# Dilated column scores: the mask is added by VectorE on the way out of the bank instead of by a TensorE product inside it

## What is computed

```
def dilated_window_attention(q, k, v, window, dilation):
    ...
    s = jnp.einsum('bnqhd,bnkhd->bnhqk', qs, kb, preferred_element_type=F32) * scale
    ...
    valid = (dist >= 0) & (dist <= n_back) & (u_key >= 0)
    s = jnp.where(valid[None, :, None], s, -jnp.inf)
    m = jnp.max(s, axis=-1, keepdims=True)
    p = jnp.exp(s - m)
    denom = jnp.sum(p, axis=-1, keepdims=True)
    o = jnp.einsum('bnhqk,bnkhd->bnqhd', (p / denom).astype(v.dtype), vb)
    lse = (m + jnp.log(denom))[..., 0]
```

## Time and profile before

| | us |
|---|---|
| median of 3 runs | 1390.65 |
| lowest, highest | 1389.37, 1392.71 |
| the profiled execution | 1388.89 |
| its span, first to last instruction | 1387.1 |
| PE busy in it | 1329.0 |
| DVE, ACT, POOL busy | 498.7, 667.5, 693.8 |
| mean granted PE clock, as a share of 2.4 GHz | 0.985 |

### The profile page before, as it was taken

One profiled execution on the slowest core, in us unless ns is written; L12 is line 12 of the kernel. 1 busy time (PEld: TensorE's weight loads), 2 busy tenths in 40 slices (PEclk: granted clock), 3 DMA queues, 4 the chain that ended last, 5 costly groups with the idle time before them and its releaser, 6 DMA issues. The chain is left out here.

```text
span 1387.1 us, 17627 instructions
## 1 busy us (share of the span) xinstructions
PE 1329.0 (96%) x6234; PEld 1037.4 (75%) x6234; DVE 498.7 (36%) x765; ACT 667.5 (48%) x1233; POOL 693.8 (50%) x571
## 2 busy tenths in 40 slices
PE   7999899988999999999999998999889999999998
PEld 6778778865677788887877786886556768888876
DVE  4675332343341222223338724114442412222221
ACT  5554423566354644554445542247644445455431
POOL 3676522354242467767447753224432425776662
PEclk9999999999999999999999999999999999999999
DMA  7553311121222243444355522112122213344432
GB/s 222 159 131 102 87 39 39 39 54 39 61 59 56 48 123 101 110 108 114 101 163 146 130 84 69 39 31 54 46 49 50 69 46 88 102 108 113 107 114 84
DMA packets 210031, 120.78 MB, mean 87 GB/s; under 512 B 9752, under 2 KB 200472, under 8 KB 209944
## 3 DMA queue, kind: packets, MB, share of 16 engines
q1 hardware_dynamic: 209944, 119.66, 32.9%
HBM read 107.04 MB, written 6.29 MB: 82 GB/s over the span
## 5 line engine op out<-in xcount | busy, mean ns | idle before, releaser
L1633 POOL TENSOR_TENSOR w_lo<-w_raw,w_hi 128x512 fp32r<-128x512 f32 (+1 forms) x404 | 501.5, 1246 | 623.5 <-ACT w_hi L1165 574.6
L747 PE MATMUL dense<-h_hi,w_hi 128*128 128x512 f32 x1168 | 502.8, 430 | 2.2 <-DVE h_lo L1346 2.1
L747 PE MATMUL dense<-h_hi,w_lo 128*128 128x512 f32 x1168 | 460.1, 394 | 0.0
L747 PE MATMUL dense<-h_lo,w_hi 128*128 128x512 f32 x1168 | 459.8, 394 | 0.0
L747 PEld LDWEIGHTS dense<-h_hi,w_hi 128*128 128x128 f32 x1168 | 222.4, 190 | 69.6 <-issue 21.9
L1165 ACT ACTIVATE w_hi<-w_raw 128x512 fp32r<-128x512 f32 (+1 forms) x401 | 232.7, 585 | 62.8 <-PE dense L747 62.6
L747 PEld LDWEIGHTS dense<-h_lo,w_hi 128*128 128x128 f32 x1168 | 222.3, 190 | 53.8 <-issue 14.4
L747 PEld LDWEIGHTS dense<-h_hi,w_lo 128*128 128x128 f32 x1168 | 221.3, 189 | 48.6
L1439 DVE TENSOR_TENSOR sig<-dense,x_rstd_row 128x512 f32<-128x512 f32 x48 | 33.2, 692 | 208.0 <-issue 122.8
L1441 DVE TENSOR_TENSOR raw<-dense,x_rstd_row 128x512 f32<-128x512 f32 x80 | 55.1, 688 | 122.4 <-PE dense L747 98.9
L1218 ACT ACTIVATE sig<-sig 128x512 f32<-128x512 f32 x48 | 30.3, 632 | 123.1 <-DVE sig L1439 123.1
(11 more groups left out here) (261 smaller groups left out, 1916.4 us busy)
## 6 DMA issues: line engine op xcount, KB each, us to landing
w_raw<-in_w_in SPq DMA_DIRECT2D x292, 256.0 KB, 2.9
w_raw<-in_w_out SPq DMA_DIRECT2D x32, 256.0 KB, 2.8
x_scratch<-v_dil SPq DMA_DIRECT2D x16, 256.0 KB, 3.4
w_raw<-in_w_mem_kv SPq DMA_DIRECT2D x16, 256.0 KB, 2.7
v_dil<-x_scratch SPq DMA_DIRECT2D x16, 256.0 KB, 2.8
turned<-normed SPq DMA_DIRECT2D x48, 64.0 KB, 2.4
inv_den<-o_norm SPq DMA_DIRECT2D x48, 64.0 KB, 2.4
silu_z<-in_mem SPq DMA_DIRECT2D x4, 512.0 KB
```

The costliest lines, as they stand in the source:

```text
L747: return nc.tensor.matmul(o, lhsT, rhs, start=start, stop=stop, skip_group_check=True)
L1633: pool.tensor_tensor(w_lo[:, g % SPLIT_SLOTS, c], w_raw[:, g % RAW_SLOTS, c], f(w_hi[:, g % SPLIT_SLOTS, c]), ALU.subtract).then_inc(w_lo_ ...
```

## The change

PE no longer issues the mask products of the dilated `col` steps; `less_maximum` ends the group and signals `col_done`. A new step on DVE waits for the `probs` slot and for `col_done`, adds the mask to the bank's scores and writes the sum into the `probs` slot: two additions per head for c = 0 (256 and 256 columns) and c = 1 (256 and 128), one of 512 for c = 2 and 3. It signals `s_masked`, which now frees the score bank. ACT waits for `s_masked` and exponentiates the slot in place. The other branches and the `row` steps keep their mask products.

```
             elif s[0] == "col":
-                score_users.append((s, p_ready, s[1:]))
+                score_users.append((s, s_masked if s[1] == DIL else p_ready, s[1:]))
                 probs_users.append((s[1:], pv_done, s[1:]))
...
-                                    less_maximum(h_, bank_[:, at:at + end - j * P], negmax_r[:, j * P:end])
-                                pairs_of = lambda ap: ap.rearrange("p (a b) -> p a b", b=P)
-                                if c == 0:
-                                    last = masked(bank_[:, :].rearrange("p (i a b) -> p i a b", i=2, b=P),
-                                                  causal_band[:, None, :, :].to_broadcast((P, 2, 2, P)))
-                                else:
-                                    masked(pairs_of(bank_[:, 0:2 * P]), causal_band)
-                                    last = masked(bank_[:, 2 * P:3 * P], rc(M_CAUSAL))
-                                last.then_inc(col_done.sem, 1)
+                                    last = less_maximum(h_, bank_[:, at:at + end - j * P], negmax_r[:, j * P:end], stop=True)
+                                    if i == 1:
+                                        last.then_inc(col_done.sem, 1)
...
-                                less_maximum(h_, by_class, strided)
-                                masked(by_class, times(rc(M_CAUSAL if g == 1 else M_COMB), STRIDE)).then_inc(col_done.sem, 1)
+                                less_maximum(h_, by_class, strided, stop=True).then_inc(col_done.sem, 1)
...
-                        wait(act, probs_ring.before(key))
-                        act.wait_ge(*col_done.of(key))
+                        if b == DIL:
+                            act.wait_ge(*s_masked.of(key))
+                        else:
+                            wait(act, probs_ring.before(key))
+                            act.wait_ge(*col_done.of(key))
...
+                        elif b == DIL:
+                            act.activation(dst, dst, ACT.Exp).then_inc(p_ready.sem, 1)
...
+                    elif kind == "col" and s[1] == DIL:
+
+                        b, h, c = key = s[1:]
+                        bank_, to = (ap.rearrange("p (a b) -> p a b", b=P)
+                                     for ap in (R[score_ring.slot(s)][:, :], probs[:, probs_ring.slot(key), :]))
+                        banded = f(rconst[:, M_CAUSAL - 2:M_BAND - 1:M_BAND - M_CAUSAL, :])
+                        causal, comb = f(rc(M_CAUSAL)), f(rc(M_COMB))
+
+                        def masked(blocks, mask):
+                            return dve.tensor_tensor(to[:, blocks, :], bank_[:, blocks, :], mask, ALU.add)
+
+                        wait(dve, probs_ring.before(key))
+                        dve.wait_ge(*col_done.of(key))
+                        if c < 2:
+                            masked(slice(0, 2), banded)
+                            last = masked(slice(2, 4), banded) if c == 0 else masked(slice(2, 3), causal[:, None, :])
+                        else:
+                            mask = causal if c == 2 else comb
+                            last = masked(slice(0, STRIDE), mask[:, None, :].to_broadcast((P, STRIDE, P)))
+                        last.then_inc(s_masked.sem, 1)
```

More of the change, by code:

```diff
@@ L484, in build @@
         p_ready = signal("p_ready", of_kind("col"))
+        s_masked = signal("s_masked", [k for k in of_kind("col") if k[0] == DIL])
         pv_done = signal("pv_done", of_kind("pv"))
@@ L805, in operand @@
                     return h_hi[:, kt, :], h_lo[:, kt, :]
-                def times(ap, n):
-                    return ap[:, None, :].to_broadcast((P, n, P))
                 def qk_there(kind, branch, idx):
@@ L996, in masked @@
                             return mm(o, rc(IDENT), blocks, stop=True)
-                        causal_band = rconst[:, M_CAUSAL - 2:M_BAND - 1:M_BAND - M_CAUSAL, :]
                         if b == FOX:
```

## The result

The changed kernel takes **1381.21 us** (median of 4 runs, 1380.15 to 1381.95), the kernel before beside it 1390.01 (4 runs, 1388.83 to 1392.71): 0.9946 of the time before, with a 95% interval of 0.9929 to 0.9964. That is 8.8 us by the medians. The four runs before are on the high side: 32 later runs of the same kernel have a median of 1388.96, 7.8 us above the change. One further run of the kernel before took 6352 us; it is left out everywhere. The profiled execution took 1380.15 us with a span of 1378.4, against 1388.89 and 1387.1.

The account below looks back on a forecast made before the run. The prediction took PE's own work to bound the kernel: 7.7 us of masks less waits of 0.65 and 0.4 gives 6.7 us gained, from the runs' median 1390.65 to 1383.9, range 1380.0 to 1388.3.

Parts of the forecast that it names:

- A mask's price: Column stages on PE: each removed mask saves its start-to-start step, 32 x 0.24 = 7.7 us less.
- Those at half clock at full-clock price: Six of the 32 mask places show 0.40 or 0.41 us at 1.2 GHz; counted at 0.24 like the others.
- Price of the additions: DVE's new additions in the column stages: 0.69 us for 512 columns, 0.41 for 256, 0.28 for 128.
- The hop's waits: PE waits for the longer DVE-then-ACT chain at pair 0, 0.6 to 0.7 us in all, and pair 6, 0.4 in all.
- reaches pair 1 at 197.99: Pair 0, layer 0: PE gets from the delayed `pv` to pair 1 in 1.56 us, at 197.99 instead of 198.12.
- Sum at equal clock: Whole kernel, clock unchanged: 7.7 us of masks less waits of 0.65 and 0.4 gives 6.7 us gained.
- the same mean clock of about 0.92: Column stages: PE's mean granted clock stays at about 0.92, as in the kernel before.
- A stretch's price: Column stages: each 3.4 us stretch at 1.2 GHz costs half its length, 1.7 us.
- Two stretches fewer, 1380.5: Rival: the shift moves the clock's falls and two fewer come, ending at 1380.5 us; chance 0.08.
- Slower, by the clock: Rival: without masks PE does less per time, the clock falls more often, six more falls give 1394.2 us; chance 0.05.
- The additions' high price: Rival: DVE's additions cost 2.4 times as much, waits take 6.1 us, ending at 1390.0; shares chance 0.11.
- hidden products: Rival: removed masks had been hidden behind weight loads, so PE gains nothing, ending at 1390; shares chance 0.11.

Follow-up runs that it names:

- no_masks: The changed kernel without masks for the dilated column scores and without DVE's additions, ACT reading the bank with scores scaled by 0.001: 1379.47 us.
- add_twice: The changed kernel with every DVE addition made twice, the second behind a signal of the first: 1386.61 us.
- room: The changed kernel with two empty places per layer moved from the end, one behind pair 0, one ahead of pair 6: 1377.17 us.
- split: The changed kernel with the 24 64-row products of pairs 2, 3 and 7 issued in two halves, one in each head's step: 1380.05 us.
- room_split: The changed kernel with both the two moved empty places per layer and the halved 64-row runs of pairs 2, 3 and 7: 1375.51 us.

## Why the prediction was right, and where it was off

Forecast was 1383.9 with 1380.0 to 1388.3; it came to 1381.2. Of the 2.7 us between them 1.7 have nothing to do with the change: the forecast subtracts its gain from 1390.65, the median of three runs, and 32 later runs have 1388.96. The gain itself, 6.7 forecast, is 7.6 between the means of the 32 runs and of the change's ten, 6.6 of it at equal clock. That 6.6 meets 6.7 so well is partly luck: in the stages the masks gave less and the waits took more than was forecast. One step was wrong, the clock that was to stay.

- **What bounds the stage**: right. Taking work from PE pays nearly in full (`no_masks`), more work on DVE costs nothing but delay, at the same two places and a little at a third (`add_twice`).
- **A mask's price**: 32 x 0.24 = 7.7 us forecast; by the stages of `no_masks` 7.1, or 0.22 each, by its runs at equal clock 7.7. "Those at half clock at full-clock price" holds well enough: had the six counted 0.40, the sum would be 8.6. By the 131 ns that the prediction took from the Trainium skill, "TensorE: Matmul & The Clock Gate", section "Back-to-back issue gap", it would be 4.2 us; the removal decides for the trace's step. The same section of the Trainium skill gives about 216 ns for a single product of 512 columns, and that agrees with the trace's 0.22.
- **Price of the additions**: right, 0.69, 0.42 and 0.28 us.
- **The hop's waits**: the places are right. Pair 6 waits 0.20 and 0.26 (0.2 forecast). At pair 0 the step "reaches pair 1 at 197.99" failed: it took 1.56 us from the `pv` to pair 1, and they are 1.73. In layer 1 the wait is 0.84 and not 0.62, although the order is the same: there the `pv` starts 0.26 us behind the end of ACT's exponential (871.47 to 871.73), in layer 0 0.10; why, no run shows. Against the 0.46 us that its masks free, pair 0 gives up 0.54 and 0.71, where 0.33 was forecast; with pair 6 that makes 1.7 us over both layers for the sum's 1.05.
- **Sum at equal clock**: 6.7 forecast. The stages give 2 x (58.1 - 55.45) = 5.3 (about 7.1 less 1.7), or 6.0 with 1.1 us for a stretch; the runs at equal clock give 6.6. What is missing may lie outside the stages, but the two executions of the kernel before differ there by 2 us once carried to an equal count (1262.6 us with five stretches, 1262.0 with six), which is too much to tell. All say that the forecast was near, and none that it was too low.
- **The clock**: forecast "the same mean clock of about 0.92"; it was 0.94. This is the step that failed, and the reason that the gain is larger than forecast. Before, a stage had 3.0 stretches, with the change 1.8 (six stages): 1.17 x 1.4 = 1.6 us per stage, 3.3 in all. Most of it doesn't stay: over all runs the mean clock went from 0.9834 to 0.9846, which is about 3.4 us less at 1.2 GHz in an execution, one stretch and not the 2.3 that the stages have lost, and worth 1.1 us; the others came back outside the stages. The balance is 2 x (62.32 - 58.02) = 8.6 us in the stages, and 7.6 between the means of all runs.
- **A stretch's price**: 1.7 forecast as half of 3.4 us, measured 1.1 to 1.4. Part of what falls into a stretch loses nothing. These are rows of the kernel before, the second head's strided subtraction, the mask behind it and the next product, all in pair 2: first in layer 0 at full clock, then in layer 1 within a stretch, with its clock. The subtraction takes 0.45 us and 0.46 from start to start, the mask 0.25 and 0.41.

```profile
207.39 0.62 PE L747 MATMUL score<-negmax_r,pick 128*128 128x512 f32 x1
207.84 0.42 PE L747 MATMUL score<-rconst 128*128 128x512 f32 x1
208.09 0.81 PE L747 MATMUL acc<-probs,v_dil 128*128 128x256 f32 x4
...
885.24 0.65 PE L747 MATMUL score<-negmax_r,pick 128*128 128x512 f32 x1
885.70 0.61 PE L747 MATMUL score<-rconst 128*128 128x512 f32 x1
886.11 1.48 PE L747 MATMUL acc<-probs,v_dil 128*128 128x256 f32 x4
```
```profile
885.00:886.00 1.00, 1.00 (x4) 0.77 (x3) 0.00 (x0) 0.46 (x1) 0.00 (x0) 0.50 0.00 0
```

- **Rivals**. "Two stretches fewer, 1380.5" (0.08) was the nearest, and deserved more. "Slower, by the clock" has the sign wrong: products left, PE waited longer, and the clock rose. The additions' high price and hidden products are refuted.

Why fewer stretches come without the masks is **open**. What is shown for the column stages is that they follow undivided runs of 24 products of 64 rows (all 48 stretches in the 24 profiled column stages start between 0.6 us before the end of such a run and 1.5 us behind it; none comes at a halved run or at a pair with c < 2) and that mask products behind the run go with more of them, with or without DVE's additions. By the Trainium skill, "TensorE: Matmul & The Clock Gate", section "What's actually happening", activity lifts the throttle and its lack brings it back. The trace doesn't read so simply here: the clock falls while PE's row is at 1.00, and in the column stages it fell more often with the products than without. Whether the time between two such runs decides, or what stands behind them, or where they fall in time by chance, no run here tells apart; `room`, which moves steps and halves nothing, has as few as `split`.

## What to carry to other kernels

On an engine that is busy all the time, as PE is here, a product that was removed gave back its start-to-start step; what the idle engine took over cost only at the places where the consumer is nearer than the new chain, and those can be found by laying the timeline of each pair beside the chain. There moving one or two steps of independent work can pay (`room`: 1.2 us beside the clock, other moved waits included). Before a difference of half a percent is put down to the edit, count the stretches of low clock in equal stages of both kernels: here they made two fifths of what the stages won. Then count the whole execution as well: there only about one of 7.6 us was the clock's. And a forecast that ends in a median should start from more than three runs where these lie 3.3 us apart.

## What the hardware showed

- In the column stages the granted clock of TensorE falls to 1.2 GHz for 3.4 us at a time while PE is busy at 1.00, always at the end of an undivided run of 24 products of 64 rows or up to 1.5 us behind it, but not behind each; such a fall costs 1.1 to 1.4 us, not 1.7.
- Fewer products or other places of work change how often it falls there: 3.2 per stage with masks on PE, 1.9 without, one in each stage of `room` and `split`, none in one stage of `room_split`. Over the whole execution the masks' removal changes it by about one in eleven.
- A subtraction of 512 columns with a step of four takes 0.44 to 0.47 us from start to start (0.52 or 0.53 where it comes first behind the 64-row products), twice the 0.23 of a contiguous product at full clock, and no more at 1.2 GHz, where the contiguous one takes 0.41.
- An addition from a score bank and an SBUF mask into SBUF takes 0.69 us for 512 columns, and ACT's exponential of 512 columns takes 0.63 us from SBUF in place of 0.59 from the bank.
